# Attention in a diffusion block: the exact exponential written over its scores in PSUM

## The reference, cut to what matters

```python
def one_block(qblk):
    s = jnp.einsum("bqkgd,bskd->bkgqs", qblk.astype(jnp.float32), kf) * scale
    p = jax.nn.softmax(s, axis=-1)
    return jnp.einsum("bkgqs,bskd->bqkgd", p, vf)
```

## Time and profile before

| | |
|---|---|
| median of 3 runs | 3093.49 us |
| lowest and highest | 3087.71 and 3096.96 us |
| span of the profiled execution | 3081.3 us |
| median less the span | 12.2 us |
| TensorE busy | 2764.0 us, 90% |
| VectorE busy | 1756.5 us, 57% |
| ScalarE busy | 1088.7 us, 35% |
| GpSimd busy | 523.6 us, 17% |

### The profile page before, as it was taken

One profiled execution on the slowest core, in us unless ns is written; L12 is line 12 of the kernel. 1 busy time (PEld: TensorE's weight loads), 2 busy tenths in 40 slices (PEclk: granted clock), 3 DMA queues, 4 the chain that ended last, 5 costly groups with the idle time before them and its releaser, 6 DMA issues. The chain is left out here.

```text
span 3081.3 us, 43080 instructions
## 1 busy us (share of the span) xinstructions
PE 2764.0 (90%) x15119; PEld 2462.6 (80%) x15119; DVE 1756.5 (57%) x2687; ACT 1088.7 (35%) x1877; POOL 523.6 (17%) x288
## 2 busy tenths in 40 slices
PE   6799999899999788998988999859599999999997
PEld 1398898898898786686686686559499999999996
DVE  0314433433533558868868868721467666666666
ACT  2222232322322326726726726720422222222223
POOL 0031221221121101011001010002032222222220
PEclk9799999999999999999999999969799999999998
DMA  8311011011011010010020020041011111111101
GB/s 294 107 56 39 15 50 38 15 50 39 15 50 45 9 46 7 0 61 7 0 61 7 0 61 0 0 174 34 28 48 41 41 41 41 41 42 46 41 27 68
DMA packets 164332, 137.69 MB, mean 45 GB/s; under 512 B 18060, under 2 KB 141484, under 8 KB 164268
## 3 DMA queue, kind: packets, MB, share of 16 engines
q1 hardware_dynamic: 151788, 111.84, 11.8%
q10 hardware_dynamic: 12480, 25.17, 2.3%
HBM read 121.52 MB, written 15.47 MB: 44 GB/s over the span
## 5 line engine op out<-in xcount | busy, mean ns | idle before, releaser
L268 PE MATMUL proj_ps<-act_hi,w_hi 128*128 128x384 f32 x1152 | 392.5, 341 | 29.6 <-ACT ri_t L490 15.9
L268 PE MATMUL up_ps<-act_hi,w_hi 128*128 128x384 f32 x1056 | 360.0, 341 | 35.0 <-ACTq L1432 33.0
L269 PE MATMUL proj_ps<-act_lo,w_hi 128*128 128x384 f32 x1152 | 389.9, 338 | 0.0
L270 PE MATMUL proj_ps<-act_hi,w_lo 128*128 128x384 f32 x1152 | 389.8, 338 | 0.0
L1489 DVE SCALAR_TENSOR_TENSOR resid_t<-down_ps,mod,resid_t 128x128 f32<-128x128 f32 x704 | 301.6, 508 | 151.9 <-PE down_ps L270 151.7
L269 PE MATMUL up_ps<-act_lo,w_hi 128*128 128x384 f32 x1056 | 359.8, 341 | 0.0
L270 PE MATMUL up_ps<-act_hi,w_lo 128*128 128x384 f32 x1056 | 359.7, 341 | 0.0
L1096 DVE TENSOR_TENSOR probs_lo<-probs,probs_hi 128x512 fp32r<-128x512 f32 x324 | 233.1, 742 | 71.1 <-ACT probs_hi L973 57.7
L1467 DVE SCALAR_TENSOR_TENSOR conv<-up,conv_t,conv 128x127 f32<-128x127 f32 (+1 forms) x176 | 217.9, 1296 | 95.0 <-ACT conv L1443 95.0
L561 DVE TENSOR_TENSOR_SCAN cum_log_f<-chunk_start,log_f 128x1152 f32<-128x1152 bf16 x16 | 49.0, 3062 | 361.7 <-ACT log_f L494 361.4
L268 PEld LDWEIGHTS proj_ps<-act_hi,w_hi 128*128 128x128 f32 x1152 | 218.4, 190 | 34.5 <-ACT ri_t L490 18.5
(11 more groups left out here) (232 smaller groups left out, 5826.1 us busy)
## 6 DMA issues: line engine op xcount, KB each, us to landing
w_raw<-in_w_in SPq DMA_DIRECT2D x64, 512.0 KB, 4.0
ada_w<-in_ada_w ACTq DMA_DIRECT2D x12, 2048.0 KB, 8.1
w_raw<-in_w_up SPq DMA_DIRECT2D x44, 512.0 KB, 3.8
w_raw<-in_w_down SPq DMA_DIRECT2D x22, 512.0 KB, 3.2
rec_scratch<-ri_t SPq DMA_DIRECT2D x8, 576.0 KB, 3.4
za_gate<-rec_scratch SPq DMA_DIRECT2D x8, 576.0 KB, 4.1
mix_scratch<-attn_t SPq DMA_DIRECT2D x8, 576.0 KB, 3.0
mix_in<-mix_scratch SPq DMA_DIRECT2D x8, 576.0 KB, 3.8
```

The lines of the kernel that those rows point to most:

```text
L268: nc.tensor.matmul(out, w_hi, x_hi, start=(k == 0), stop=False)
L269: nc.tensor.matmul(out, w_hi, x_lo, start=False, stop=False)
L270: return nc.tensor.matmul(out, w_lo, x_hi, start=False, stop=last)
```

## The change

The rounded exponential is computed first. The full-precision one then reads the same bank and is written over the scores in it, and carries `ex_done`. The subtraction reads the bank in place of `probs`, and the tile `probs` is gone. So S(k) now waits for `lo_done` of block k-2 (the bank is in use until then), and ScalarE's own wait for `lo_done` is dropped.

```diff
-        PE32 = sb("probs", [P, 2, 512])
...
-                        wait_step(ex_done, NC, max(g - 1, 0) + 1, o, 10)
+                        wait_step(lo_done, NC, max(g - 1, 0) + 1, o, 10)
...
-                        wait_step(lo_done, NC, max(g - 1, 0) + 1, o, 10)
-
-                        nc.scalar.activation(PE32[:, slot(n, i), :], ps[:, B_ST + slot(n, i), :], ACT.Exp, scale=HEAD ** -0.5)
                         if g >= 4:
                             wait_step(pv_done, NC, g - 3, o, 10)
-                        nc.scalar.activation(PH[:, split_slot(n, i), :], ps[:, B_ST + slot(n, i), :], ACT.Exp, scale=HEAD ** -0.5).then_inc(ex_done, 1)
+                        bank = ps[:, B_ST + slot(n, i), :]
+                        nc.scalar.activation(PH[:, split_slot(n, i), :], bank, ACT.Exp, scale=HEAD ** -0.5)
+                        nc.scalar.activation(bank, bank, ACT.Exp, scale=HEAD ** -0.5).then_inc(ex_done, 1)
...
-                        nc.vector.tensor_tensor(PL[:, s, :], PE32[:, slot(n, i), :], PH[:, s, :].bitcast(F32), ALU.subtract).then_inc(lo_done, 1)
+                        nc.vector.tensor_tensor(PL[:, s, :], ps[:, B_ST + slot(n, i), :], PH[:, s, :].bitcast(F32), ALU.subtract).then_inc(lo_done, 1)
```

## The result

The changed kernel takes 3105.74 us (median of 5 runs, 3104.28 to 3109.0) against 3093.49 us before (median of 5 runs by now, 3086.75 to 3096.96). The ratio of the runs is 1.0052, with a 95% interval of 1.0035 to 1.0068: slower by about half a per cent. The quotient of the two medians, 1.0040, lies within that interval.

What follows compares the result with a forecast made beforehand. VectorE was taken to bound the middle of attention steps, so ScalarE's idle time is free. Later steps +20.6, last +6.4, first -9.1, exponential -2 gave +16 us on the median 3093.49: 3109.5 us, range 3100 to 3125.

Steps and rivals of the forecast that it cites:

- The walk through a step: Second to seventh attention step of each head: scores wait for low parts, +0.86 us per step, 24 steps, +20.6 us.
- M1: VectorE's first row maximum in a later attention step: starts 6.36 us after `put_max`, was 5.94, +0.42.
- M3: VectorE's third row maximum in a later attention step: starts 13.63 us after `put_max`, was 13.01, +0.6.
- L(8): Low part of block 8 in a later attention step: ready 15.87 us after `put_max`; VectorE could take it at 15.6.
- The last step: Each head's last attention step, without row maxima: 17.1 us in place of 15.51, four heads, +6.4 us.
- The first step: Each head's first attention step, beside GpSimd: low parts no longer stretched, 19.9 us each, -9.1 us over four heads.
- The price of the low part: VectorE's subtraction with one input in PSUM: no difference taken; the skill's rule would put +10 us on the sum.
- The price of the exponential in place: ScalarE's second exponential, PSUM to PSUM: up to 36 ns cheaper, 3.9 us in all; half taken, -2 us.
- The base: Whole kernel: profiled span 3081.3 us, 12.2 under the median 3093.49, taken as what surrounds every execution.
- relief without cost: Attention: TensorE's later scores cost nothing, only first steps shrink; -12.5 us, 3081; chance 0.04.
- stretched low parts that stay: First steps: low-part pairs stay at 4.3 and 3.4 us beside GpSimd; +28 us, 3121; chance 0.08.
- dearer and cheaper operands: Low part a tenth longer: 3119.5, chance 0.07; exponential 0.3 us dearer: 3141, 0.06; 0.1 us shorter: 3100, 0.12.

Runs made afterwards that it cites:

- wait_only: Kernel before with only the change's waits: scores wait for the low part, ScalarE's own wait dropped, operands stay in SBUF; ratio to before 1.0108.
- pool_late: Kernel before with one added GpSimd wait: in the first three heads its splits start only after query tile 3; ratio to before 1.0016.
- order_only: Kernel before with the two exponentials in the other order, `ex_done` moving with the second, nothing else changed; ratio to before 0.9993.
- first_four: Kernel before with the exponential in place in PSUM only for four blocks of each head's first step, rounded exponential first everywhere; ratio to before 0.9953.

## Why the prediction was right

The direction, the mechanism and nearly all sizes held. That the sum came out within 1 us is in part luck: two terms of it were wrong, by 2.5 and 2 us, in opposite directions. Point by point:

- **The walk through a step.** Predicted and measured starts after `put_max` (the step at 1929.27 above): M1 6.36 and 6.27, M3 13.63 and 13.49, L(8) 15.87 and 15.76, the next `put_max` 18.87 and 18.77. About 0.1 us too long from M1 on: S starts 0.05 us after a low part, where I took 0.09, and M1 0.77 after X1, where I took 0.83. The first could have been read before: in the step of the earlier trace rows, X3 started at 1922.11, 0.05 us after M2 ended. Over 24 steps the loss is 18.1 us (18.81 less 18.06, each), forecast 20.6, so this term was 2.5 us too large.
- **The last step**: 17.13 in all heads, forecast 17.1; 4 x 1.62 = 6.5 us, forecast 6.4. The rounds are as forecast too: from L(4) on they took 2.64, 2.64 and 2.63 us, forecast 2.65.
- **The first step**: 19.85 to 19.88, forecast 19.9; together 9.3 us less, forecast 9.1. No low part of the changed kernel is over 694 ns. wait_only and pool_late show both halves of the reason: with the operands in SBUF the stretch stays, and it goes where GpSimd goes.
- **The price of the low part**: none, as taken (a mean of 688 ns against 690 for an undisturbed one before). The rule of the Trainium skill that I had weighed against it (VectorE: DVE Perf Modes, The TRN2 errata), 65 ns more for a PSUM source, did not show.
- **The price of the exponential in place**: a mean of 594 ns and a median of 593. Its fair partner is the same exponential of order_only, also the second of its pair, but written to SBUF: a median of 592. So the destination makes no difference here. This term of the sum was wrong: my -2 us for a faster destination was not there; nor was a double length. The Trainium skill (ScalarE: Activation LUTs, Step-by-step) has PSUM as the faster destination; these two rows show no gain.
- **The sum**: the attention steps give 18.1 + 6.5 - 9.3 = +15.3 us, forecast +16, and the ratio 1.0052 is +16 us. Without the -2, the forecast would have been +17.9; the gain that did not exist covered most of the 2.5 us by which the later steps were taken too long.
- **The base.** This step failed. I took the 12.2 us between the profiled span and the median for what surrounds every execution. The execution profiled of the changed kernel had a span of 3107.2 us and took 3109.0, so 1.8 us surround it, and 1.8 to 1.9 in every other run on record. With 1.8 us the profiled execution of before took about 3083.1, so it was one of the shorter ones: 46 later executions of that kernel, on two chips, took 3078.53 to 3098.08. Span against span the kernels differ by 25.9 us: 15.3 from these steps of attention, 7.1 from ahead of them (1147.87 against 1154.95), where no instruction was changed, 0.8 between the heads and 2.7 behind attention. The reason that I gave for the base was wrong, and it did no harm, because the +16 was in the end added to the median. The shift of the medians, +12.3, lies within the spread of the runs around +16.

The rivals: relief without cost falls with wait_only, which has the cost alone; stretched low parts that stay fall with the 694 ns; dearer and cheaper operands fall with the rows of L1094 and L971. The lines behind them, by line: the low parts before and in the changed kernel, the exponential in place, and its partner of order_only (duration ns min/median/max, first and last start).

```profile
L1096 DVE TENSOR_TENSOR probs_lo<-probs,probs_hi x324: 670/685/2881, 1152.2 to 1997.8; 128x512 fp32r<-128x512 f32 x162
...
L1094 DVE TENSOR_TENSOR probs_lo<-att_ps,probs_hi x324: 671/691/694, 1159.4 to 2021.0; 128x512 fp32r<-128x512 f32 x162
...
L971 ACT ACTIVATE att_ps<-att_ps x324: 589/593/603, 1158.8 to 2020.3; 128x512 f32<-128x512 f32 x162
...
L973 ACT ACTIVATE probs<-att_ps x324: 588/592/662, 1150.5 to 1994.6; 128x512 f32<-128x512 f32 x162
```

## What to carry to other kernels

When a buffer is given up, look at which engine the freed-up wait moves to and what stands behind it in that engine's queue: here the same semaphore cost nothing on ScalarE and 0.75 us a step at the head of TensorE's queue, and 0.57 of that went when the independent matmuls were put ahead of the waiting one. A gain that exists in one stage only (an operand in PSUM beside a busy GpSimd) is best taken in that stage only: first_four kept the relief and paid the wait for four blocks in place of 81. And an idle time of an engine that is not on the path, as the 131 us of ScalarE here, is no sum to be won.

## What the runs showed of the hardware that I had not expected

I had spoken of instructions with both inputs in SBUF. In pool_late an instruction with one input is stretched too: L1088, four columns, took 2.27 us in place of 0.17, and the copy L1073 2.46 beside GpSimd's subtraction. The trace of before had a sign of it: in the first head's first step, the copy L1072 took 0.88 us, and in pool_late, with GpSimd away, 0.29. A low part with one input in PSUM and one in SBUF was not stretched. The Trainium skill (SBUF — State Buffer, Who interferes with whom) has both: copies, casts and `tensor_scalar` can use the port that VectorE shares with GpSimd, a two-input operation with at most one input in SBUF doesn't. The traces agree.

A stretched low part also went together with a lower clock where TensorE waited for it. In wait_only, after idle times of 2.59 to 2.73 us, matmuls ran at 0.63 us in place of 0.40, and the first steps of three heads had 0.86 of the clock; in the changed kernel all four had 1.00 and took the same time within 0.03 us. In the kernel before, TensorE was idle for 1.87 to 1.91 us at the like place in three heads, and the clock fell in one of them. So the idle time alone does not say whether it falls.

How much of wait_only's 1.7 to 2.0 us beyond my walk is clock no run separates, but the rows allow an estimate for the first head. M2 started there at 1179.94, 2.33 us after S(5) at 1177.61. At the upper clock X stands 0.58 behind S, and M starts 0.77 behind X (1941.38, 1941.96 and, for X1, 1934.77 to 1935.54 in the changed kernel), together 1.35: 1.0 us less. From M2 to the next `put_max` it took 9.57 us, and 8.77 in the fourth head of the same run, at 1.00: another 0.8. So by this estimate the clock is about all of the 1.7 us.
